# Delta rule's projections: a second buffer for the split weights, key products in six steps, the block inversion between the gate's casts

## The reference, cut to what matters

```
proj = x @ w_in                      # 1024 -> 3072 (q, k, v) + 1024 (z, the gate) + 16
qkv  = silu(causal conv of width 4 along the tokens)
q, k, v = split(qkv)                 # 8 heads of 128 each
lower = strict_lower(k beta k^T * decay)        # per head and block of tokens
attn  = (q k^T) * decay
sol   = inverse(1 + lower) applied to v and k   # the delta rule
o     = rms_norm(o) * silu(z)
```

## Time and profile before

| what | us |
|---|---|
| median of 3 runs | 2197.71 (2196.98 to 2200.77) |
| profiled execution, its own time | 2189.83 |
| its span | 2188.0 |
| PE busy | 2002.9 (92%) |
| DVE busy | 1483.9 (68%) |
| ACT busy | 1301.5 (59%) |
| block `gdn_projections` in the trace | 0 to about 272 |

### The profile page before, as it was taken

One profiled execution on the slowest core, in us unless ns is written; L12 is line 12 of the kernel. 1 busy time (PEld: TensorE's weight loads), 2 busy tenths in 40 slices (PEclk: granted clock), 3 DMA queues, 4 the chain that ended last, 5 costly groups with the idle time before them and its releaser, 6 DMA issues. The chain is left out here.

```text
span 2188.0 us, 33544 instructions
## 1 busy us (share of the span) xinstructions
PE 2002.9 (92%) x9013; PEld 1499.7 (69%) x9013; DVE 1483.9 (68%) x2487; ACT 1301.5 (59%) x2151; POOL 400.9 (18%) x309
## 2 busy tenths in 40 slices
PE   8889878989999999999984999998999999999994
PEld 6667678747777677777763655766767667777772
DVE  3566746567888778878763226656778777888884
ACT  3444355226877778777762224425767777777774
POOL 0000041002222222222223000001322222222221
PEclk9999989999999999999996999999999999999997
DMA  5310032067999999999992210156999999999994
GB/s 190 129 58 20 1 105 102 34 234 291 371 370 366 353 351 381 366 364 365 345 308 85 77 58 1 54 186 240 369 337 366 358 338 359 363 368 374 369 364 131
DMA packets 181033, 541.72 MB, mean 248 GB/s; under 512 B 26432, under 2 KB 57568, under 8 KB 180832
## 3 DMA queue, kind: packets, MB, share of 16 engines
q1 hardware_dynamic: 150688, 460.65, 56.2%
q0 software_dynamic: 25248, 69.25, 12.6%
q10 hardware_dynamic: 5024, 10.91, 1.3%
HBM read 506.75 MB, written 54.10 MB: 256 GB/s over the span
## 5 line engine op out<-in xcount | busy, mean ns | idle before, releaser
L1770 DVE TENSOR_TENSOR gu_l<-ring,gu_h 128x1024 fp32r<-128x1024 f32 x512 | 610.8, 1221 | 90.0 <-ACT gu_h L1634 79.2
L1634 ACT CAST gu_h<-ring 128x1024 fp32r<-128x1024 f32 x512 | 523.5, 1061 | 80.3 <-DMA ring<-in_moe_w_up 64.6
L1549 PE MATMUL bank<-gu_h,xgT_l 128*128 128x512 f32 x1024 | 413.6, 404 | 0.0
L1551 PE MATMUL bank<-gu_h,xgT_h 128*128 128x512 f32 x1024 | 401.3, 392 | 0.0
L1550 PE MATMUL bank<-gu_l,xgT_h 128*128 128x512 f32 x1024 | 400.4, 391 | 0.0
L1898 POOL DMA_INDIRECT xg<-h_rows,list_idx x128 | 148.8, 1162 | 911.8 <-issue 482.4
L1601 PE MATMUL bank<-ring,hmT_f 128*128 128x512 f32 x536 | 273.3, 591 | 0.0
L1641 ACT CAST down_h<-ring 128x1024 fp32r<-128x1024 f32 x128 | 134.1, 1048 | 224.3 <-DMA ring<-in_moe_w_down 128.0
L1776 DVE TENSOR_TENSOR down_l<-ring,down_h 128x1024 fp32r<-128x1024 f32 x128 | 156.9, 1225 | 106.5 <-ACT down_h L1641 100.4
L1917 POOL DMA_INDIRECT moe_sum<-y,out_idx x128 | 193.2, 1510 | 163.1 <-issue 150.9
L1551 PEld LDWEIGHTS bank<-gu_h,xgT_h 128*128 128x128 f32 x1024 | 192.9, 188 | 42.3
(11 more groups left out here) (376 smaller groups left out, 3038.2 us busy)
## 6 DMA issues: line engine op xcount, KB each, us to landing
ring<-in_moe_w_gate SPq DMA_DIRECT2D x256, 512.0 KB
ring<-in_moe_w_up SPq DMA_DIRECT2D x256, 512.0 KB
ring<-in_moe_w_down SPq DMA_DIRECT2D x256, 512.0 KB
ring<-in_a_w_in SPq DMA_DIRECT2D x32, 512.0 KB
ring<-in_x SPq DMA_DIRECT2D x8, 512.0 KB, 5.6
ring<-in_a_w_out SPq DMA_DIRECT2D x8, 512.0 KB
h_rows<-ring ACTq DMA_DIRECT2D x8, 512.0 KB, 2.6
moe_sum<-y ACTq DMA_DIRECT2D x8, 512.0 KB, 6.8
```

The lines of the kernel that those rows point to most:

```text
L1549: nc.tensor.matmul(out, lhsT=xl, rhs=wh, start=k == 0, stop=False)
L1551: last = nc.tensor.matmul(out, lhsT=xh, rhs=wh, start=False, stop=k == KD - 1)
L1634: nc.scalar.copy(gu_h[:, c, :, :], gate_up_cols(gate_slot, c * CH // 2, CH // 2)).then_inc(gu_hi.sem, 1)
L1770: nc.vector.tensor_tensor(gu_l[:, c, :, :], gate_up_cols(gate_slot, c * CH // 2, CH // 2), gu_h[:, c, :, :].bitcast(F32), ALU.subtract).th ...
```

## The change

1. **Second buffer.** For the odd steps c < 17 the split weights lie in a second pair of tiles, in slot 10 of the ring (free until the first decayed unit is written there). The cast of step c then waits for step c - 2 in place of c - 1. ACT casts both parts of step c + 2 in its loop c; DVE makes the low part 1 behind the convolution of step c.
2. **Three units a step.** The 16 units are spread as 3, 3, 3, 3, 3, 1 over steps 17 to 22; none is left behind step 23.
3. **Packing.** `pack` is cut in four calls of two copies: behind steps 20 and 21 for the first half, behind the silu of step 22 and behind the cast of z 1 for the second.
4. **z 0 and z 1.** Their casts come ahead of the silu of steps 22 and 23 on ACT and ahead of the convolution of step 23 on DVE. z n = 2 is cast before `systems`, n = 3 inside it.
5. **Elimination.** A cast of z after every 2.0 us of estimated elimination up to n = 9, then after every 3.9; then X's part of the inverse (L831, L833 before), one cast, Y's part (L832, L834), the rest; `copy_sums` behind the cast of n = 14.
6. **Banks.** z uses the PSUM banks in another order, the sums bank 1 for bank 4; so `keys_T(0, g)` of the next block must wait for two gate activations, and both stand behind `product5(0, g)`.

```diff
+        TWO_DEEP = 2 * H + 1
+        second_h, second_l = (ring_r[:, 10, BLOCK * j:BLOCK * j + BLOCK].rearrange("p (a k q) -> p a k q", a=2, q=P) for j in range(2))
+        def split_of(c):
+            return (second_h, second_l) if c < TWO_DEEP and c % 2 else (qkv_h[:, :, :, :], qkv_l[:, :, :, :])
 act_qkv_hi:
-                if c >= 1 and part == 0:
-                    act.wait_ge(first_half_used.sem, first_half_used.base + c)
-                elif c >= 1:
-                    act.wait_ge(qkv_ready.sem, qkv_ready.base + c)
+                used = c - 1 if c < TWO_DEEP else c
+                if used >= 1 and part == 0:
+                    act.wait_ge(first_half_used.sem, first_half_used.base + used)
+                elif used >= 1:
+                    act.wait_ge(qkv_ready.sem, qkv_ready.base + used)
-            return bank[(4, 5, 0, 1, 3, 7, 2, 6)[TT * half + tt]]
+            return bank[(1, 2, 3, 5, 4, 0, 7, 6)[TT * half + tt]]
+        def kq_units(c):
+            first = 3 * (c - 1 - 2 * H)
+            return range(min(first, KQ_UNITS), min(first + 3, KQ_UNITS))
 ScalarE, loop over c:
-                    if c + 1 < N_QKV:
+                    if TWO_DEEP <= c + 1 < N_QKV:
                         act_qkv_hi(act, c + 1, [1])
                     if c + 2 < N_QKV:
-                        act_qkv_hi(act, c + 2, [0])
+                        act_qkv_hi(act, c + 2, range(2) if c + 2 < TWO_DEEP else [0])
+                    elif c + 2 == N_QKV:
+                        act_z_hi(act, 0)
+                    else:
+                        act_z_hi(act, 1)
+                        pack(1, 1)
                     act.wait_ge(conv_done.sem, conv_done.base + c + 1)
...
+                    elif c in (N_QKV - 4, N_QKV - 3):
+                        pack(0, c - N_QKV + 4)
                     elif c == N_QKV - 2:
-                        pack(0)
-                act_z_hi(act, 0)
+                        pack(1, 0)
                 copy_v(H - 2)
-                act_z_hi(act, 1)
-                pack(1)
+                act_z_hi(act, 2)
                 copy_v(H - 1)
 VectorE, loop over c:
-                    if c + 1 < N_QKV:
+                    if TWO_DEEP <= c + 1 < N_QKV:
                         dve_qkv_lo(v, c + 1, [1])
+                    elif c + 1 == N_QKV:
+                        dve_z_lo(v, 0)
+                        dve_z_lo(v, 1)
                     v.wait_ge(qkv_ready.sem, qkv_ready.base + c + 1)
...
                     ins.then_inc(conv_done.sem, 1)
+                    if c + 2 < TWO_DEEP:
+                        dve_qkv_lo(v, c + 2, [1])
                     if c > 2 * H:
-                        decayed(2 * (c - 1 - 2 * H))
-                        decayed(2 * (c - 1 - 2 * H) + 1)
+                        for u in kq_units(c):
+                            decayed(u)
...
-                systems()
-                low, spent = 2, 1.8
+                systems(lambda: dve_z_lo(v, 3))
+                low, spent = 4, 0.0
                 for j in range(SUB - 1):
-                    while low < KD + 6 and spent >= 1.8:
+                    room = 2.0 if low < KD + 2 else 3.9
+                    if spent >= room:
                         dve_z_lo(v, low)
-                        low, spent = low + 1, spent - 1.8
+                        low, spent = low + 1, spent - room
                     eliminate(j)
                     spent += 0.4 + 0.00208 * (SUB - 1 - j) * (j + 1)
-                for n in range(low, KD + 6):
+                inverse(X_sys.rearrange("p (c i) -> p i c", i=SUB), X_sys, 8)
+                dve_z_lo(v, low)
+                inverse(Y_sys.rearrange("p (i c) -> p i c", c=SUB), Y_sys, 9)
+                for n in range(low + 1, 2 * KD):
                     dve_z_lo(v, n)
-                copy_sums()
-                dve_z_lo(v, KD + 6)
-                dve_z_lo(v, KD + 7)
-                inverses()
+                    if n == KD + 6:
+                        copy_sums()
                 norms()
 gdn_delta_rule, TensorE:
-                        if tt < 0:
-                            keys_T(0, g)
-                        elif tt > 0:
+                        if tt > 0:
                             from_state(tt, g)
                         if ahead:
                             product5(tt + 1, g)
+                    for g in range(2) if tt < 0 else ():
+                        pe.wait_ge(z_done.sem, z_done.base + 2 * TT - 2)
+                        keys_T(0, g)
```

More of the change, by code:

```diff
@@ L494, in act_qkv_hi @@
                     unit_wait(act, c // 2)
[L495 to L499 removed]
+                used = c - 1 if c < TWO_DEEP else c
[3 more added lines that the diff above has]
+                    act.wait_ge(qkv_ready.sem, qkv_ready.base + used)
+                nc.scalar.copy(split_of(c)[0][:, part, :, :], qkv_cols(c, part)).then_inc(qkv_w_hi.sem, 1)
         def dve_qkv_lo(v, c, parts):
@@ L613, in decays, with pack @@
                     nc.scalar.activation(sym[:, 2 * half:2 * half + 2, :, :], sym[:, 2 * half:2 * half + 2, :, :], ACT.Exp, scale=-1.0).then_inc(sym_done.sem, 1)
-                def pack(half):
+                def pack(half, part):
                     act.wait_ge(kq_done.sem, kq_done.base + 2 * KQ_PAIRS * (half + 1))
-                    for b in range(QUADS):
+                    act.wait_ge(qkv_w_lo.sem, qkv_w_lo.base + 2 * (N_QKV - 2))
+                    for b in (2 * part, 2 * part + 1):
                         dst = packed[quad(b), :, 2 * H * half:2 * H * (half + 1)]
@@ L654, in _ @@
                             decays((c - 9) // 4)
+                    elif c in (N_QKV - 4, N_QKV - 3):
+                        pack(0, c - N_QKV + 4)
                     elif c == N_QKV - 2:
-                        pack(0)
-                act_z_hi(act, 0)
+                        pack(1, 0)
                 copy_v(H - 2)
-                act_z_hi(act, 1)
-                pack(1)
+                act_z_hi(act, 2)
                 copy_v(H - 1)
-                for n in range(2, 2 * KD):
+                for n in range(3, 2 * KD):
                     if n >= KD + 4:
@@ L717, in sum_squares @@
                         pe.wait_ge(z_done.sem, z_done.base + 1)
-                    nc.tensor.matmul(bank[4][:, :], lhsT=one_row[:, 2 * H - 1 - c:2 * H - 1 - c + P], rhs=squares[:, c % 2, :], start=c == 0, stop=c == H - 1).then_inc(sums_ready.sem, 1)
+                    nc.tensor.matmul(bank[1][:, :], lhsT=one_row[:, 2 * H - 1 - c:2 * H - 1 - c + P], rhs=squares[:, c % 2, :], start=c == 0, stop=c == H - 1).then_inc(sums_ready.sem, 1)
                 def transpose_sums():
@@ L722, in transpose_sums @@
                     for tt in range(TT):
-                        last = nc.tensor.transpose(bank[4][:, tt * P:(tt + 1) * P], sums[:, tt * P:(tt + 1) * P], ident)
+                        last = nc.tensor.transpose(bank[1][:, tt * P:(tt + 1) * P], sums[:, tt * P:(tt + 1) * P], ident)
                     last.then_inc(sums_ready.sem, 1)
@@ L729, in _ @@
                     out = qkv_bank[c % 3][:, :]
+                    high, low = split_of(c)
                     for part in range(2):
@@ L733, in _ @@
                             k = 4 * part + j
-                            nc.tensor.matmul(out, lhsT=qkv_l[:, part, j, :], rhs=hT_h[:, k, :], start=k == 0, stop=False)
-                            nc.tensor.matmul(out, lhsT=qkv_h[:, part, j, :], rhs=hT_l[:, k, :], start=False, stop=False)
-                            last = nc.tensor.matmul(out, lhsT=qkv_h[:, part, j, :], rhs=hT_h[:, k, :], start=False, stop=k == KD - 1)
+                            nc.tensor.matmul(out, lhsT=low[:, part, j, :], rhs=hT_h[:, k, :], start=k == 0, stop=False)
+                            nc.tensor.matmul(out, lhsT=high[:, part, j, :], rhs=hT_l[:, k, :], start=False, stop=False)
+                            last = nc.tensor.matmul(out, lhsT=high[:, part, j, :], rhs=hT_h[:, k, :], start=False, stop=k == KD - 1)
                         last.then_inc(qkv_ready.sem if part else first_half_used.sem, 1)
@@ L741, in _ @@
                         transpose_v(c - 1 - 2 * H)
[L742 to L745, removed]
+                        for u in kq_units(c):
+                            keys_queries(u)
                 for n in range(2 * KD):
@@ L750, in _ @@
                         if k == 0 and half == 0 and tt == 0:
+                            pe.wait_ge(kq_done.sem, kq_done.base + KQ_UNITS)
+                        elif k == 0 and tt == TT - 1 and half == 0:
+                            pe.wait_ge(conv_done.sem, conv_done.base + N_QKV - 1)
+                        elif k == 0 and tt == 1 and half == 1:
                             pe.wait_ge(conv_done.sem, conv_done.base + N_QKV)
-                        elif k == 0 and half == 0 and tt == TT - 1:
-                            pe.wait_ge(kq_done.sem, kq_done.base + KQ_UNITS)
                         elif k == 0 and half == 1 and tt == 0:
@@ L809, in decayed, with systems @@
```

(5 more changed lines are left out.)

25 lines of the change are left out of this document (10 added, 15 removed).

## The result

| kernel | median us | lowest to highest | own time of the profiled execution | span |
|---|---|---|---|---|
| before | 2197.35 (4 runs) | 2195.25 to 2200.77 | 2189.83 | 2188.0 |
| after | 2172.95 | 2168.78 to 3384.06 (4 runs) | 2171.31 | 2169.5 |

The changed kernel takes 0.9889 of the time before (95% interval 0.9873 to 0.9905), 24.4 us less between the medians of the table; the profiled executions are 18.5 apart. The forecast was 2178.6 in 2171 to 2187.

What follows compares the result with a forecast made beforehand. PE was taken to bound the block, held up by DVE's waits for ACT's casts. Steps 3 to 22 (-19.0), tail (-0.7) and next block (+0.6) sum to -19.1; 2197.71 - 19.1 = 2178.6 us, range 2171 to 2187.

Steps and rivals of the forecast that it cites:

- Steps 3 to 16: Fourteen steps on PE: the second buffer removes stalls, small waits and lower clock, 98.43 to 76.3 us, -22.1.
- Rival 1: Second buffer doesn't cover long work on ACT; three stalls and slow clock stay, -5.7 for -22.1, time 2195.0; chance 0.07.
- rival 4: PE without pauses is held at 1.2 GHz in the steps, 4.8 us more a step, up to 2246; chance 0.03.
- Steps 17 to 22: Steps with three units each: 16 units for 12, +3.1 us, so 53.15 for 50.07.
- The tail: From the start S of step 23 to the next block: two new stalls, old z 14 stall gone, -0.7 us.
- first stall: In the tail, PE stands at the transposes of head 7 behind z 0: a new stall of 4.5 us.
- second stall: In the tail, PE waits for DVE's cast of z 12: a new stall of 3.2 us.
- the clock behind that stall: In the tail, low PE clock behind the stall before z 12: 1.1 us, being 1.6 at two in three.
- Rival 2: Tail worse: DVE falls behind at z 4 to z 10, seven times 1 us, 2185.6; chance 0.11.
- Rival 3: Tail better: pack or DVE faster than laid out, 2173 to 2175; chance 0.09.
- The next block: One more key transpose on PE behind the products and ahead of `inverse5`: +0.6 us (0.3 to 1.1).
- rival 5: The gain is lost later, in a stage that waits for loads: about 2197.7; chance 0.02.

Runs made afterwards that it cites:

- part 1 alone: The second buffer for odd steps under 17 and nothing else of the change, against the kernel before: 2173.29 us, ratio 0.9897.
- edits of ACT's and DVE's order: Two separate edits of the changed kernel: ACT's cast of z 1 ahead of `pack(1, 0)`, 2172.29 us; DVE's casts of z moved between the inverse's parts, 2173.29 us.
- keys first: Changed kernel with `keys_T(0, 0)` and `keys_T(0, 1)` of the next block ahead of its first products: one execution of 2174.97 us.
- one buffer: Changed kernel with its second buffer used for step 1 alone, all other parts kept: 2197.0 us, ratio 1.0005 to the kernel before.
- second pair: Second traces of the kernel before and the changed kernel, no edit, on another chip: medians there 2196.04 and 2173.19 us.
- first stall's edit: Changed kernel with ACT's cast of z 1 ahead of `pack(1, 0)` and `pack(1, 1)` behind the cast of z 2: 2172.29 us, ratio 0.99.
- three edits: Changed kernel with z 1's cast ahead of the packs, z casts between the inverse's parts, and keys ahead of products: 2168.0 us, then 2165.47 on another chip.
- before again: The kernel before, no edit, profiled a second time on another chip: one execution of 2193.32 us.
- after; again: The changed kernel, no edit, traced and timed a second time on another chip: 2173.19 us, ratio 0.9899.

## Why the prediction was right

**Steps 3 to 16: -22.1, measured 98.43 to 76.29, -22.1.** The pace of PE from starts (5.45 a step), the stalls that all go, the clock that follows, the 0.6 us to spare behind step 9: each as worked out. The two experiments on part 1 show the cause from both sides. With the buffer (in two different kernels) no stall and clock 1.00; without it, three stalls of 2.40, 3.85 and 3.88 and clock 0.93. Rival 1 (long work on ACT is not covered) is refuted, and so is rival 4 (a steady PE held at the low level): all fourteen steps ran at the full clock.

**Steps 17 to 22: 53.15, measured 183.81 - 130.33 = 53.48.** Four units more cost 3.4 us, not 3.1. The kernel with part 1 alone keeps 50.0.

**The tail: -0.7, measured -2.4.** The mechanism was right. The first stall was put at 4.5 and is 4.24, the start of the elimination at S + 21.4 and is at 205.63 - 183.81 = 21.8. The edits of ACT's and DVE's order shorten the first stall to 2.0 and remove the second, as their causes say. Two terms were too large.

The first is the second stall, put at 3.2 and measured at 2.53. PE came to it as forecast (S + 51.4 for 51.6), but the low part of z 12 was ready 0.9 earlier, at S + 53.9 for 54.8. Most of that was in the addition: the start 21.4, the eliminations 23.5, eight casts 5.2, X's part 3.31 and the cast of z 12, 0.65, make 54.1. The small waits at z 4 and z 10, put at 1.8 us together, are 0.10 and 0.60, but they stand ahead of this stall and go into its length, not into the end of the tail.

The second is the clock behind that stall. I had given it 1.1 us, 1.6 at two in three, and in the two traces of this kernel it stayed full. The 0.9 and the 1.1, less 0.3 by which the last products took longer, are the 1.7 us. That the clock stayed full is chance: in the kernel with the keys first the same stall cost the 1.6. The four traces with this tail took 69.67, 69.63, 70.59 (one buffer) and 71.30, the three with the old one 72.07, 72.94 and 72.04, so the means are 2.1 apart.

Rival 2 (waits at every cast of z) is refuted: the 0.60 is the only gap above half a microsecond among the products of z beside the second stall. Rival 3 (a better tail) is half true: DVE was 0.9 faster than laid out.

**The next block: +0.6, measured +1.0.** Inside its bounds of 0.3 to 1.1, near the top of them; the two groups of traces put the order of keys and products at 1.1.

**From the block to the time.** All parts together were -19.1 and are -20.2 in the trace, and rival 5 (the gain is lost later) is refuted: the rest of the span is the same within its scatter. The medians are 26.0 apart on the first chip (2197.35 and 2171.31) and 22.9 on the second, so 3 to 6 us more than the -20.2 (and 2 more than the -20.8 of the second pair) of the block. The two pairs of traces put the difference in the rest at -0.4 and +0.7; where the others lie isn't shown.

The forecast of 2178.6 is 5.6 above the median of the table and 7.3 above the 2171.31. Nearly all of it is one term. For the profiled execution the sum gave 2170.7, and it took 2171.31. But the median was then put 7.9 above the profiled execution, as for the kernel before, and it lies 1.6 above it or less. The 7.9 belonged to one short execution of the kernel before: 2189.83 us, where its runs took 2195.25 to 2200.77, and its second trace lay 2.7 under the median of its chip. So the median falls outside the 2175.5 to 2182 that the forecast had as its own range, and under the 2173 to 2175 of rival 3. That the wide range still takes it in, close to its low end, is in part luck; the right place and size of the gain, in the block, is not.

**What the prediction didn't say.** It summed the parts, and so didn't set them apart by worth. Its own numbers had it: part 1 is -22.1, the rest +3.0. Measured, the rest is +2.2 in the block (+2.7 to +3.3 without the second buffer) and nothing in the time.

## What to carry to other kernels

Where an engine in the middle of a chain has long side work, look at how far ahead its product is made, not at how long it takes: one more buffer, in a ring slot that was free, removed 10 us of stalls, 6 us of small waits and restarts and the 6 us of clock behind them. When work is reordered in a list written out by hand, count for each engine what stands ahead of the instruction that another engine waits for; the two stalls that this change brought were to be seen in advance, and moving a few lines halved the first and took out the second. Small gains in a stretch are to be judged in the stretch: below 3 us the whole time doesn't tell them from scatter, and edits that each show nothing may show together.

## What the runs showed of the hardware

**The clock behind an idle gap is not certain.** The table gives PE's idle gaps in this block and how many passes behind them were 0.427 us apart and not 0.227:

| gap, us | slow passes behind it, one number for each execution |
|---|---|
| 2.01 to 2.02 (first stall's edit; three edits, twice) | 0, 0, 0 |
| 2.40 (before; before again; without the buffer) | 8, 0, 0 |
| 2.51 to 2.54 (after; again; without the buffer; first stall's edit; keys first) | 0, 0, 0, 5, 4 (and the sums behind them at half the rate) |
| 3.72 to 4.25 (all kernels that have one) | 6 to 12 behind each of fourteen |

The page "TensorE: Matmul & The Clock Gate" of the Trainium skill (HAM oscillation) tells of a kernel in which waits of some 3 to 5 us for DMA stand between groups of products, and the half clock comes back behind every one of them. The last line agrees, fourteen times of fourteen. The shorter gaps of the lines above are not that case: at 2.01 nothing was slow, and between 2.4 and 2.54 us the same gap did both, in three executions of eight slow and in five not. Where it was slow it cost 1.6 us each time (8 passes at 0.2; or z 12 from 4.2 to 5.8 us with its sums). A forecast of such a gap should carry the 1.6 us as a chance, and not as a price.

**A table switch on ACT costs the load alone.** The load at 98.02 starts 0.02 us behind the instruction ahead of it (96.73 + 1.27), takes 1.28, and the exponential starts at 99.31, 0.01 later. The page "ScalarE: Activation LUTs" of the Trainium skill (What ACT_TABLE_LOAD costs) gives some 1.38 us of draining at each switch beside the load. No trace here shows it, ahead of a load or behind one with work waiting. With it the 0.60 to spare would have been a stall, by an estimate from the page's figure.
